# One core, two transformer blocks: the next weight tile taken token tile by token tile at three norms, and linear attention reordered

## The reference, cut to what matters

```
for l in range(2):
    mix = diff_moba_mixer(x, ...) if l == 0 else gla_mixer(x, ...)
    x = layer_norm(ALPHA * x + mix, ln_mix_g[l], ln_mix_b[l])
    x = layer_norm(ALPHA * x + square(relu(x @ w1[l])) @ w2[l], ln_ffn_g[l], ln_ffn_b[l])
```

## Time and profile before

| | |
|---|---|
| median of 3 runs | 1714.73 us (1711.41 to 1714.90) |
| the profiled execution's own time | 1713.44 us |
| its span from first to last instruction | 1711.6 us |
| mean granted TensorE clock | 0.94 of 2.4 GHz |
| TensorE busy | 1380.6 us, 81% |
| VectorE busy | 1131.3 us, 66% |
| ScalarE busy | 539.2 us, 32% |
| GpSimd busy | 454.7 us, 27% |

### The profile page before, as it was taken

One profiled execution on the slowest core, in us unless ns is written; L12 is line 12 of the kernel. 1 busy time (PEld: TensorE's weight loads), 2 busy tenths in 40 slices (PEclk: granted clock), 3 DMA queues, 4 the chain that ended last, 5 costly groups with the idle time before them and its releaser, 6 DMA issues.

```text
span 1711.6 us, 17345 instructions
## 1 busy us (share of the span) xinstructions
PE 1380.6 (81%) x6264; PEld 971.9 (57%) x6264; DVE 1131.3 (66%) x2051; ACT 539.2 (32%) x1023; POOL 454.7 (27%) x393
## 2 busy tenths in 40 slices
PE   6976788777777677777777788658999899789998
PEld 5875668523223232222222267547999687679996
DVE  6655665688887788886555556647756659577564
ACT  2453434222221213212111233323434246234341
POOL 1154305244443443544444200000211025001110
PEclk9988899999998999999999989878999999889999
DMA  9554526799999999999999823204555534245550
GB/s 367 190 184 148 196 74 227 293 421 409 421 421 412 421 408 382 400 422 420 422 421 421 344 75 123 98 25 142 182 196 197 189 110 147 75 151 179 188 197 25
DMA packets 116629, 433.17 MB, mean 253 GB/s; under 512 B 6832, under 2 KB 7088, under 8 KB 83520
## 3 DMA queue, kind: packets, MB, share of 16 engines
q0 software_dynamic: 36864, 268.45, 38.0%
q1 hardware_dynamic: 79392, 162.51, 26.8%
q10 hardware_dynamic: 288, 1.11, 0.2%
HBM read 431.00 MB, written 1.05 MB: 252 GB/s over the span
## 4 chain that ended last, share of the span: by engine, by line
PE 47%; DMA 23%; DVE 19%; ACT 6%; issue 2%; POOL 2%; SPq 0%; DVEq 0%; ACTq 0%; POOLq 0%
PE PS L45 45%; DMA EB<-in_experts,EI 22%; DVE EB L78 5%; DVE WL L75 3%; ACT BIG L24 2%; PE PS L84 1%; DVE X L63 1%; POOL W L75 1%; ACT WH L24 1%; DVE Y L75 1%; DMA W<-in_w_ada 1%; DVE GV L75 1%; DVE EB L63 1%; DVE XL L75 1%; DVE ST L69 1%
## 5 line engine op out<-in xcount | busy, mean ns | idle before, releaser
L45 PE MATMUL PS<-EB,BIG 128*128 128x512 f32 x1024 | 495.4, 628 | 169.9 <-ACT BIG L24 169.8
L45 PEld LDWEIGHTS PS<-EB,BIG 128*128 128x128 f32 x1024 | 190.3, 197 | 470.3 <-ACT BIG L24 287.3
L78 DVE CUSTOM_DVE_ANT_0 EB<-EB,Y 128x1024 f32<-128x1024 f32 x256 | 313.4, 1224 | 146.0 <-DMA EB<-in_experts,EI 145.0
L39 POOL DMA_INDIRECT EB<-in_experts,EI x256 | 288.3, 1126 | 397.0 <-PE PS L45 380.9
L75 DVE TENSOR_TENSOR WL<-W,WH 128x1024 fp32r<-128x1024 f32 x228 | 297.5, 1351 | 109.5 <-ACT WH L24 109.3
L45 PE MATMUL PS<-XH,WH 128*128 128x256 f32 x928 | 272.0, 293 | 12.8 <-DVE WL L75 10.0
L24 ACT ACTIVATE WH<-W 128x1024 fp32r<-128x1024 f32 x240 | 237.8, 1047 | 91.8 <-PE PS L45 84.9
L45 PE MATMUL PS<-XL,WH 128*128 128x256 f32 x928 | 265.0, 286 | 0.0
L45 PE MATMUL PS<-XH,WL 128*128 128x256 f32 x928 | 265.0, 286 | 0.0
L45 PEld LDWEIGHTS PS<-XH,WH 128*128 128x128 f32 x928 | 180.9, 195 | 17.9 <-DVE WL L75 11.1
L45 PEld LDWEIGHTS PS<-XL,WH 128*128 128x128 f32 x928 | 180.8, 195 | 2.7 <-issue 2.4
(11 more groups left out here) (170 smaller groups left out, 1512.1 us busy)
## 6 DMA issues: line engine op xcount, KB each, us to landing
W<-in_ffn_w SPq DMA_DIRECT2D x32, 2048.0 KB, 8.8
W<-in_w_ada SPq DMA_DIRECT2D x12, 2048.0 KB, 12.2
W<-in_w_in SPq DMA_DIRECT2D x6, 2048.0 KB, 12.9
W<-in_hy_w_in SPq DMA_DIRECT2D x6, 2048.0 KB, 13.5
W<-in_gla_w_in SPq DMA_DIRECT2D x6, 2048.0 KB, 7.9
W<-in_w_query SPq DMA_DIRECT2D x4, 2048.0 KB, 8.2
W<-in_w_out SPq DMA_DIRECT2D x2, 2048.0 KB, 8.3
EB<-in_experts,EI POOLq DMA_INDIRECT x256, 11.1
```

The costliest lines, as they stand in the source:

```text
L39: return lambda e: e.indirect_dma_start(*a, **k)
L45: return lambda e: e.matmul(*a, **k)
L78: return lambda e: e.tensor_tensor_reduce(*a, **k)
```

## The change

1. After the norm of either mixer, the first up tile of the feed-forward part (`up[0, 0]`) is no longer an `fm_tile`. The new `both_tiles` makes it token-major: the product of token tile 0 (24 products), then `before.last()` (the turn of token tile 1), then the product of token tile 1. `give(..., turn=False)` keeps the turn out of the norm. ReLU and square are taken token-major, and 8 transposes (`turn_tokens`) bring the result to `AH` and `AL` during the next tile.
2. After the norm of the first feed-forward part the q tile is treated alike, and turned by 8 transposes (`turn_query`) after the gate sums. The decay columns come after it. `both_tiles` has no `tick` in it, where `fm_tile` had four `tick(2)`.
3. The first step of `levels` stands ahead of the turn of q and of the k tile (it stood behind the k tile).
4. The value tiles come ahead of the gate tiles (also in the order of the weight transfers). Of the last gate tile's second token tile only half of the 24 products is made before the heads, the rest after them; its silu and its multiplication follow the squares of the heads.
5. The heads' norm, their turn and the product with w_out go token tile by token tile.
6. `bank()` passes over a PSUM bank that `fm_tile` is still filling.

```diff
@@ plan
-        gla_in = {j: wplan_on(A["gla_w_in_2"], 0, j) for j in (0, 1, 4, 5, 2, 3)}
+        gla_in = {j: wplan_on(A["gla_w_in_2"], 0, j) for j in range(6)}
@@ new
+        def both_tiles(tile, before, evac=lambda t, b, tk: None):
+            done = []
+            for t in range(2):
+                if t:
+                    before.last()
+                b = bank()
+                tk = dense(PS[b][:, :], take(tile), tm_pairs(tile, t), before.xt[t], *bank_free[b])
+                if t:
+                    wdone(tile, tk)
+                done.append(evac(t, b, tk))
+            return done
@@ ffn
+            def square_tokens(t, b, tk):
+                r = Y[:, 0, t * 512:(t + 1) * 512]
+                td = dve(lambda e: e.tensor_scalar(r, PS[b][:, :], 0.0, None, ALU.max), tk, *at_free[0])
+                bank_free[b] = (td,)
+                return r, act(lambda e: e.activation(r, r, ACT.Square), td)
+            def turn_tokens(t):
...
+                for c in range(4):
+                    tk = tr(PS[b][:, c * 128:(c + 1) * 128], r[:, c * 128:(c + 1) * 128], ta, *bank_free[b])
...
+                th = act(lambda e: e.activation(hi, ps, ACT.Copy), tk, *at_free[0], ordered=False)
+                tl = dve(lambda e: e.tensor_tensor(lo, ps, hi.bitcast(F32), ALU.subtract), th, ordered=False)
...
+            squares = both_tiles(up[0, 0], before, square_tokens)
...
-                        fm_tile(up[g, j], ev, *t_xt)
+                        fm_tile(up[g, j], ev, *t_xt, hook=turn_next)
@@ linear attention
+        t_query = both_tiles(gla_in[0], norm, evac_query)
+        t_xt = norm.tokens
         b = bank()
         tk = narrow(b, wg_parts[0], *t_xt)
...
-        fm_tile(gla_in[0], evac_flat(0, 128.0 ** -0.5), *t_xt)
         t_bg2 = gate_sums()
-        fm_tile(gla_in[1], evac_flat(1024, 1.0))
+        lv = levels()
+        next(lv)
+        for t in range(2):
+            e_free[0] = e_free[1] = (turn_query(t),)
+        fm_tile(gla_in[1], evac_flat(1024, 1.0), *t_xt)
         t_qk = act.last
-        lv = levels()
         next(lv)
...
         for j in range(2):
-            tm_tile(gla_in[4 + j], with_levels(evac_silu(j)), n=2)
-        for j in range(2):
             tm_tile(gla_in[2 + j], with_levels(evac_tok(lambda t: VG[:, t, j * 512:(j + 1) * 512])), n=2)
+        t_v = (act.last, dve.last)
+        tm_tile(gla_in[4], with_levels(evac_silu(0)), n=2)
+        last_gate = take(gla_in[5])
+        b = bank()
+        tk = dense(PS[b][:, :], last_gate, tm_pairs(last_gate, 0), *bank_free[b])
+        bank_free[b] = with_levels(evac_silu(1))(b, 0, tk)
+        t_sg = [pool.last]
+        tick(2)
+        b_gate = bank()
+        dense(PS[b_gate][:, :], last_gate, tm_pairs(last_gate, 1), *bank_free[b_gate], ks=range(4), stop=False)
+        tick(2)
         for _ in lv:
             pass
+        t_am = dve.last
...
-                t_heads.append(mm(PS[b][:, (h % 2) * 256:(h % 2 + 1) * 256], pairs, *t_v, *bank_free[b]))
+                t_heads.append(mm(PS[b][:, (h % 2) * 256:(h % 2 + 1) * 256], pairs, *t_v, t_am, *bank_free[b]))
+        tk_gate = dense(PS[b_gate][:, :], last_gate, tm_pairs(last_gate, 1), ks=range(4, 8), start=False)
...
+        ready = head_norm(0, head_squares(0))
+        t_square = head_squares(1)
+        bank_free[b_gate] = evac_silu(1)(b_gate, 1, tk_gate)
...
+        x_heads = [turn_tile(Y[:, 0, :], 0, ready)]
+        ready = head_norm(1, t_square)
...
+            if t == 0:
+                x_heads.append(turn_tile(Y[:, 1, :], 1, ready))
+                for j in range(2):
+                    norm_mix.give(j, first[j][0], 0, first[j][1])
+                    tick(2)
```

More of the change, by code:

```diff
@@ L233, in build @@
         turn = [0]
+        filling = set()
         def bank():
+            while turn[0] % 4 in filling:
+                turn[0] += 1
             b = turn[0] % 4
@@ L528, in fm_tile @@
                 b = bank()
+                filling.add(b)
                 for j in range(2):
@@ L559, in close_pair @@
                         wdone(pair[j], tk)
-                    norm.give(j, b, t, tk)
+                    norm.give(j, b, t, tk, turn=False)
                     if (j, t) != (1, 1):
                         tick(n)
+        def both_tiles(tile, before, evac=lambda t, b, tk: None):
[9 more added lines that the diff above has]
+            return done
         def log_exp_tables():
@@ L1646, in layer_norm, with ffn @@
             return Normed(piece, stats, apply, X, turned=not last)
-        def ffn(l, t_xt, norm, beside=None):
+        def ffn(l, before, norm, beside=None):
             up, down = ffn_tiles[l]
@@ L1691, in close_mixer @@
             close_pair(pair, norm, *t_xt)
-            return norm.tokens
-        t_xt = close_mixer(0, hy_out, t_xt)
+            return norm
+        norm_mix = close_mixer(0, hy_out, t_xt)
         f = (pe.last, dve.last, act.last)
@@ L1701, in build @@
         norm = layer_norm(A["ln_ffn_g_2"][0], A["ln_ffn_b_2"][0])
-        ffn(0, t_xt, norm, beside=lambda free: wg_parts.append(narrow_parts(wg, 16, 0, t_wg, *free)))
-        t_xt = norm.tokens
+        ffn(0, norm_mix, norm, beside=lambda free: wg_parts.append(narrow_parts(wg, 16, 0, t_wg, *free)))
         f = (dve.last, act.last)
@@ L1717, in build, with turn_query @@
         bank_free[b] = (ta,)
+        def turn_query(t):
+            b = bank()
+            for c in range(4):
+                tk = tr(PS[b][:, c * 128:(c + 1) * 128], QT2[:, t, c * 128:(c + 1) * 128], t_query[t], *bank_free[b])
+            ta = act(lambda e: e.activation(QG.rearrange("p (h t) -> p h t", h=4)[:, :, t * 128:(t + 1) * 128],
+                                            PS[b][:, :].rearrange("p (h t) -> p h t", h=4), ACT.Copy), tk, ordered=False)
+            bank_free[b] = (ta,)
+            return tk
         ZG, LG = Y[:, 0, :], Y[:, 1, :]
```

60 lines of the change are left out of this document (47 added, 13 removed).

## The result

The changed kernel takes 1728.85 us (median of 5 runs, 1726.20 to 1732.32) against 1714.73 before; the ratio is 1.0088, 95% interval 1.0062 to 1.0114. It is slower by 14 us (0.9%). The forecast of 1723.3 us, 9.9 us on top of the profiled execution of the kernel before and 8.6 on top of the median, had the sign, most of the places and about two thirds of the size. The profiled execution took 1726.2 us with a span of 1724.4.

The account below looks back on a forecast made before the run. TensorE, busy 81% of the span, was taken as the bound through its idle time, clock and added passes. On 1713.4 us profiled: -2.2 first norm, +7.8 heads' start, -0.6 behind the heads, +4.9 clock, giving 1723.3 us; range 1712 to 1731.

Parts of the forecast that it names:

- First norm: First mixer norm to the end of the second up tile: long waits for the norm nearly filled, gain 2.2 us.
- k tile: After the second norm: TensorE waits 13.7 us for late weight pieces, loses 1.1 to the clock, tile 9.6 us late.
- clock term: Low TensorE clock behind the new waits between the norms and the end: 4.9 us in all, bounds 0 and 10.
- the levels win it back: Rival: VectorE bounds the levels, so the heads start 3.1 us later, not 7.8; 1715.3 us, chance 0.13.
- pieces not late: Rival: the k tile's pieces are ready in time, heads 3.5 us earlier than before; 1709.6 us, chance 0.12.
- more than that: Rival: clock falls at every new wait (+10) and VectorE bounds the levels at 8.1 us each; 1732 us, chance 0.15.
- Ahead of the diagonal: Between the k tile and the diagonal: only k's copy is waited for, 0.8 us with its latency.
- Levels and heads: Levels at 7.38 us each, VectorE's load hidden or nearly; TensorE idles 6 us before the heads, which start 7.8 later.
- Heads to the second up tile: Heads through w_out and the third norm to the second up tile's end: +76.3 us against +76.9, gain 0.6.

Follow-up runs that it names:

- e4: The kernel before with only the token-major first up tile at the norms of both mixers; 1706.84 us, ratio 0.9944 to the kernel before.
- e7: e3 with the old end of the linear attention and, replacing the early k-tile pieces, a two-piece tick before token tile 1's ReLU or copy; 1701.32 us.
- e1: The changed kernel with the first step of the levels moved back behind the k tile; 1716.89 us, ratio 1.0006 to the kernel before.
- e3: The changed kernel with the k tile's last two pieces ahead of the decay columns and the first level behind the k tile; 1709.00 us.
- e8: e7 with token tile 0's ReLU and square (or copy) behind token tile 1's turn, and the diagonal and levels waiting for k's copy alone; 1700.57 us.
- e2: The changed kernel with the k tile's last two weight pieces queued ahead of the decay columns; 1714.44 us, ratio 0.9990 to the kernel before.

## Why the prediction was right, and where it was off

**First norm: right.** Forecast a gain of 2.2 us with waits of 1.3, 2.7 and 2.85; measured 2.45 with 1.29, 2.49 and 2.25 + 0.17. e4 and e7 confirm the parts.

**k tile: right.** Forecast a wait of 13.7 + 0.1, measured 13.02 + 0.33; GpSimd's pair at 2.2, measured 2.16; k's end 9.6 us late, measured 10.65 (49.76 us after the stop, before 39.11). The clock was at the low level on the way out, 0.50 from 1394 to 1400, and that was mis-sized: I took 1.1 us. From the end of the wait to the end of the tile the trace has 13.34 us at a mean clock of 0.77, where 84 of 96 passes at the full clock take 9.8, so the low clock cost about 3 us. The sum in the prediction is 0.7 too high as it stands (1400.0 + 0.1 + 9.8 + 1.1 is 1411.0, not 1411.7), and the wait ended 0.5 us earlier than forecast. It is luck that these two took away half of what the clock term lacked. e1 to e3 show the cause by taking it away from either side, and with it fell the rivals "the levels win it back" and "pieces not late". The third, "more than that", is wrong in its half on VectorE (diagonal to heads took 66.71 us, before 66.91) and nearly right in its half on the clock (see the clock term below).

**Ahead of the diagonal: missed.** The step "its copy (0.8 with its latency)" was wrong: the wait was 2.58, since `act.last` had come to name two weight pieces behind the copy. I had the order of ScalarE's queue and took the token for the copy's. This is 1.9 us.

**Levels and heads: right.** The wait ahead of the last level's products was put at 1.3 and was 1.34, the one ahead of the heads at 6 and was 5.89. That VectorE would keep up was right too, until the diagonal came 18.5 us earlier after the stop (e8); at 16.5 us earlier (e3) the first level's operands are 0.35 us late. The forecast of the heads' start, 7.8 us late, became 12.3 by the k tile's extra 1.1, the diagonal's 1.9 and about 1.7 of clock behind the diagonal (the window at 1410.70 below).

**Heads to the second up tile: right at the full clock.** First w_out product at +15.1, measured +14.89; third norm's waits at 4.1 and 2.7, measured 3.81 and 2.38. The 3.81 hangs on the execution: with the same code it is 2.41 to 2.44 in e1, e2 and e3, where the clock had fallen before (last section).

**The clock term: too small.** I took 4.9 us. These are the changed kernel's stretches at 0.50 outside the k tile and the heads, ahead of 1547 us (the heads ran at the low clock in both kernels, 7.99 and 8.16 us):

```profile
1410.70:1414.10 3.40, 3.40 (x16) 3.21 (x16) 3.10 (x5) 3.31 (x4) 0.00 (x0) 0.50 1.05 405
...
1492.60:1496.00 3.40, 3.40 (x10) 2.65 (x9) 2.18 (x6) 0.00 (x0) 0.00 (x0) 0.50 0.70 267
1523.30:1530.10 6.80, 5.80 (x14) 4.56 (x15) 6.24 (x14) 0.41 (x2) 0.00 (x0) 0.50 0.65 248
1536.90:1540.40 3.50, 3.50 (x10) 2.72 (x9) 0.00 (x0) 0.00 (x0) 0.00 (x0) 0.51 0.02 5
```

Half of TensorE's busy time in them is lost: 1.7 + 1.7 + 2.9 + 1.75 = 8.1 us, and a further 1.7 behind the wait of 2.25 at 1547, so twice the term and about its upper bound of 10. This is a comparison with my sum, which put the new pieces at the full clock, and not with the kernel before: that one lost 1.5 us at the third norm, and more than 2 at the start of its w_out product (0.50 from 1487.2 to 1491.8, where TensorE is busy all the time), whose length my sum took over as measured. Between the two kernels the clock makes about 2 of the 15.5 us; the others are idle time and added transposes, as the windows above show. By the marks the forecast's +5.0 (-2.2, +7.8, -0.6) became -2.45 to down 1, +12.34 to the heads and +5.68 to down 2. The mechanisms stand; what was mis-sized is the clock term, the k tile's share of the low clock, and the wait ahead of the diagonal. The measured median, 1728.85, lies just beyond the 1718 to 1728 that I gave to the forecast's own mechanism, and inside the whole range (1712 to 1731).

**Open.** Medians moved more than the traces in e1 (12 against 10.6 us of the second block, of which 6.2 by the queue) and e4 (9 against 5.7). One profiled execution of each kernel can't tell where that lies. The mean granted clock of every execution is on record, and the time hardly follows it: among the kernel before's 20 executions of the first session the correlation is -0.1, among e1's ten -0.5, among e3's five +0.2. The start of the first mark, which moves by up to 9 us between the profiled executions, is the larger candidate, but it is known for one execution of each kernel alone.

## What to carry to other kernels

A step moved ahead in the program is moved ahead in every engine's queue: before it is moved, name what stands behind its first instruction that waits, on each engine, and who waits for that. A helper that issues background work (here `tick`) is part of the loop that calls it; where a loop is replaced, its background work needs a new place (in e7 the two pieces behind the token-major product, ahead of its ReLU, brought no new wait). A wait on "the newest instruction of the queue" silently takes in whatever was put behind the one that is meant. And a forecast that sets a new stretch at the full clock against an old one as measured compares two clocks: what the old one lost has to be taken out first.

## What the runs showed of the hardware that I had not expected

The clock's answer to waits of 2 to 4 us differs between places and executions. In the changed kernel it stayed at 1.00 through 2.49 and 2.25 us at the first norm (1170 to 1200 us), and fell behind the same waits at the third (2.38 at 1536, 2.25 at 1547). The stretch from the heads to down 2 took 101.06, 101.05 and 100.51 us in e1, e2 and e3 and 105.23 in the changed kernel, with the same code. Where the clock falls decides what it costs. In e1 and e3 it fell behind the 2.46 us wait in the last w_out product (0.51 from 1502.9 to 1506.3 in e1), TensorE reached the third norm later, and the next wait was shorter:

```profile
1517.89 0.50 PE L45 MATMUL PS<-WH,XH 128*128 128x512 f32 x1 [2.41 <-DVE XL L75]
```

It was at 1.00 from 1506.5 to 1526 there. In the changed kernel it stayed at 1.00 through the same product (1508.0 to 1520.4), TensorE waited 3.81 us instead, and behind that wait it was at 0.50 for 6.8 us. So 1.7 us lost ahead of a wait that another engine ends cost almost nothing, and full speed up to that wait was followed by a loss of 2.9 us. For a change of a few microseconds such a stretch must be read at several executions or corrected by the granted clock.

A weight piece on VectorE cost 1.16 us beside an idle GpSimd (4.63 us for four at 1403 us in the changed kernel) and 1.78 on average where GpSimd subtracted for most of the time (14.23 us for eight in e8, GpSimd busy for 11.8 of them), and GpSimd's pair 2.16 against 3.92: GpSimd's pair differed by 1.8 us with what VectorE did beside it, which is as much as many a wait above.
